# One layer of a hybrid decoder with mixture of experts, one core: last tile projected in column halves and its logits scaled late, GpSimd's end moved into the last branch, counts ahead of a table product, idle products behind a pair

## What is computed

```python
h = rmsnorm(x, g_mix)
a_b, a_c, a_x, p_x, c_a, c_g, d_u, d_v = split(h @ w_in, 8)      # 1024 -> 2048
mix = concat([short_conv(..), pooling(..), conv31(..), chunk_gating(..)])
x = x + mix @ w_out                                            # 1024 -> 1024
h = rmsnorm(x, g_ffn)
lg, le = h @ rg_w + rg_b, h @ re_w + re_b                      # 4 groups, 32 experts
g = argmax(lg);  e1, e2 = top2(le within g);  w2 = softmax(v2) * softmax(lg)[g]
x = x + sum_k w2[k] * ((silu(h @ w_gate[e_k]) * (h @ w_up[e_k])) @ w_down[e_k])
y = rmsnorm(x, g_final)
```

## Time and profile before

| | |
|---|---|
| runs, us | 647.76, 646.43, 646.13; median 646.43 |
| profiled execution, us | 649.03 |
| its span, us | 647.3 |
| mean granted clock of TensorE | 0.958 |
| busy: PE, DVE, ACT, POOL | 92%, 74%, 44%, 16% |
| chain that ended last | PE 58%, DVE 17%, DMA 2%, ACT 2%, issue 2% |

### The profile page before, as it was taken

How to read it: one execution, slowest core, us unless ns; L and a number is a source line. 1 busy time by engine, 2 the same in 40 slices (tenths; PEclk the granted TensorE clock), 3 DMA queues, 4 the chain that set the end, 5 groups by cost and what they waited for, 6 DMA issues and landing times.

```text
span 647.3 us, 10611 instructions
## 1 busy us (share of the span) xinstructions
PE 594.5 (92%) x3527; PEld 509.6 (79%) x3527; DVE 481.2 (74%) x752; ACT 283.6 (44%) x437; POOL 106.0 (16%) x150
## 2 busy tenths in 40 slices
PE   5899999999999998999999934999999999998792
PEld 3899999997898897888888724888888888885641
DVE  4947997999999678366665666878888878885287
ACT  5642112330313345322221134777777777774433
POOL 4300001000000000000000003133344444452000
PEclk9799999999999999999999955999999999999798
DMA  8660210111203103544221097799999999941595
GB/s 312 127 127 22 66 33 11 56 55 34 65 10 132 65 2 131 194 173 185 72 91 50 33 331 217 224 345 357 335 331 368 393 383 377 380 181 57 190 418 225
DMA packets 51303, 115.83 MB, mean 179 GB/s; under 512 B 8419, under 2 KB 26728, under 8 KB 50153
## 3 DMA queue, kind: packets, MB, share of 16 engines
q1 hardware_dynamic: 42757, 92.30, 41.4%
q0 software_dynamic: 6656, 17.84, 8.0%
q10 hardware_dynamic: 1828, 4.96, 2.0%
HBM read 99.23 MB, written 20.68 MB: 185 GB/s over the span
## 4 chain that ended last, share of the span: by engine, by line
PE 58%; DVE 17%; DMA 2%; ACT 2%; issue 2%; POOL 0%; SPq 0%; POOLq 0%; DVEq 0%; ACTq 0%
PE ps L1976 14%; PE ps L2094 9%; PE ps L1799 8%; PE ps L2073 5%; PE ps L2054 5%; PE ps L2072 5%; PE ps L2074 5%; PE ps L2017 2%; DVE at_mixP L1247 2%; DVE at_x L1722 2%; DVE at_hT L1206 1%; PE ps L1750 1%; DVE at_x L1707 1%; DVE at_lnsq L1432 1%; DMA at_opair_p<-scratch_out 1%
## 5 line engine op out<-in xcount | busy, mean ns | idle before, releaser
L1799 PE MATMUL ps<-at_hT,at_ring 128*128 128x384 f32 x936 | 165.7, 333 | 1.1 <-ACT at_wk L645 1.1
L1799 PEld LDWEIGHTS ps<-at_hT,at_ring 128*128 128x128 f32 x936 | 155.9, 188 | 6.5 <-issue 5.0
L1976 PE MATMUL ps<-at_hT,at_mring 128*128 128x512 f32 (+1 forms) x432 | 102.6, 393 | 1.9 <-DVE at_mring L1400 1.1
L1976 PEld LDWEIGHTS ps<-at_hT,at_mring 128*128 128x128 f32 (+1 forms) x432 | 77.3, 182 | 21.1 <-DVE at_mring L1400 1.6
L2072 PE MATMUL ps<-at_whi,at_hTm 128*128 128x256 f32 x280 | 82.0, 293 | 0.0
L2074 PE MATMUL ps<-at_whi,at_hTm_lo 128*128 128x256 f32 x280 | 79.0, 282 | 0.0
L1247 DVE SCALAR_TENSOR_TENSOR at_mixP<-at_uc,sb_par,at_mixP 128x1024 f32<-128x1024 f32 x60 | 77.3, 1289 | 2.1
L1594 DVE TENSOR_TENSOR at_hTm_lo<-ps,at_hTm 128x1024 fp32r<-128x1024 f32 x35 | 42.9, 1225 | 21.6 <-ACT at_hTm L885 21.6
L2054 PEld LDWEIGHTS ps<-sb_ident,at_xg 128*128 128x128 f32 x280 | 37.3, 190 | 24.8 <-issue 22.0
L1601 DVE TENSOR_TENSOR at_wlater_lo<-at_wlater,at_whi 128x1024 fp32r<-128x1024 f32 x40 | 49.0, 1226 | 9.7 <-ACT at_whi L893 7.5
L2072 PEld LDWEIGHTS ps<-at_whi,at_hTm 128*128 128x128 f32 x280 | 53.8, 192 | 0.2 <-issue 0.2
(11 more groups left out here) (255 smaller groups left out, 901.3 us busy)
## 6 DMA issues: line engine op xcount, KB each, us to landing
at_wlater<-in_expert_w_gate SPq DMA_DIRECT2D x20, 512.0 KB
at_wlater<-in_expert_w_up SPq DMA_DIRECT2D x20, 512.0 KB
at_wlater<-in_expert_w_down SPq DMA_DIRECT2D x20, 512.0 KB
at_raw<-in_w_in SPq DMA_DIRECT2D x16, 512.0 KB, 3.9
at_opair_p<-scratch_out SPq DMA_DIRECT2D x8, 1024.0 KB, 14.0
at_wfirst<-in_expert_w_gate SPq DMA_DIRECT2D x15, 512.0 KB
at_wfirst<-in_expert_w_up SPq DMA_DIRECT2D x15, 512.0 KB
at_wfirst<-in_expert_w_down SPq DMA_DIRECT2D x15, 512.0 KB
```

Source lines behind the costliest of these rows:

```text
L1799: mm = pe.matmul(ps[:, bank + r, 0:t1 - t0], w[:, wpart, k * P:(k + 1) * P], hT[:, hpart, k, t0:t1], start=(m, wpart, hpart) == (0, 0, 0), ...
L1976: mm = pe.matmul(ps[0:n, b + r, :], mring[:, 1 - i % 2, mpart, k * P:k * P + n], wo[:, wpart, k, r * 512:(r + 1) * 512], start=(c, mpart, ...
```

## The change

1. **Last tile in column halves.** For the last tile `project` runs all channels into the first 512 columns and then all into the second (`o_half` after the first). VectorE's `last_half` adds 512 columns to x and multiplies them with the gain, without the root; the transposes wait for `last_scaled`, the end of the second half. The logits are multiplied with the root in `route`. ScalarE makes the scaled rows for the store, in another buffer, and fills all four gather buffers behind that.
2. **VectorE's list** is written out for the end: row and column selectors are apart, and the column selectors of tile 7 stand behind the choice of the last tile.
3. **Counts** of the last tile stand ahead of the table product of tile 7 on TensorE.
4. **Rows of expert 1** are transposed into banks 5 and 6 (`rows_psum`), and its transposes no longer wait for the remainder of expert 0's rows.
5. **Last overflow block**: the branch is asked ahead of D of the block before; in it, TensorE runs half of that D, the transpose, the other half, and the last D; ScalarE copies the transpose ahead of the output.
6. **GpSimd's end**: the memset with `moe_done` stands in `all_scattered`, inside the branches.
7. **Idle products**: the last 8 of 32 wait for the pair of the sample's tile.

```diff
@@ -378 +378 @@
+def rows_psum(b):
+    n = 5 if isinstance(b, int) and b == 1 else 0
+    return ps[:, n:n + 2, :]
...
 def by_tile(flat):
@@ -537 +542 @@
     def store_h2(i):
...
-        sp.dma_start(hs[i * P:i * P + rows(i), :], wk[0:rows(i), i % 2, 0:D])\
+        sp.dma_start(hs[i * P:i * P + rows(i), :], wk[0:rows(i), 2 if i == LAST else i % 2, 0:D])\
@@ -864 +869 @@
-        if i >= LAST:
-            act.wait_ge(s["o_done"], TILES)
-            for n in range(3) if i == LAST else range(3, XG):
-                zeros = ones[:].unsqueeze(1).broadcast_to([P, KC, P])
-                do(A(xg[:, n, :].rearrange("p (k t) -> p k t", k=KC), zeros, ACT.Copy, scale=0.0),
-                   s["xg_zero"])
+    act.wait_ge(s["rs_ready"], 2 * TILES)
+    do(A(wk[0:NS, 2, 0:D], wk[0:NS, LAST % 2, 0:D], ACT.Copy, scale=rs[0:NS, 1, LAST:TILES]),
+       s["h2_ready"])
+    for n in range(XG):
+        zeros = ones[:].unsqueeze(1).broadcast_to([P, KC, P])
+        do(A(xg[:, n, :].rearrange("p (k t) -> p k t", k=KC), zeros, ACT.Copy, scale=0.0),
+           s["xg_zero"])
@@ -881 +886 @@
-        src = ps[:, 0:2, :].rearrange("p b (k t) -> p (b k) t", t=P)
+        src = rows_psum(b).rearrange("p b (k t) -> p (b k) t", t=P)
...
     def expert_whi(i, j, h):
@@ -971 +976 @@
                     with act.If(i * LAP + j + 1 < total):
...
-                    expert_out(i + NE // LAP, j - 1)
                     with act.If(i * LAP + j + 2 > total):
...
+                        expert_out(i + NE // LAP, j - 1)
...
+                    with act.Else():
+                        expert_out(i + NE // LAP, j - 1)
...
     def final_root(i):
@@ -1154 +1161 @@
+        g.memset(gcol[:, 0:1], 0).then_inc(s["moe_done"], 1)
...
     def over_from(o):
@@ -1170 +1178 @@
-    do(g.memset(gcol[:, 0:1], 0), s["moe_done"])
@@ -1473 +1480 @@
+    def last_half(h):
+        if h == 0:
+            dve.wait_ge(x_in[LAST], 32)
+            dve.wait_ge(s["o_half"], 1)
+            dve.wait_ge(s["t2_done"], LAST - 1)
+            dve.wait_ge(h2_stored[LAST % 2], 16 * (LAST // 2))
+        else:
+            dve.wait_ge(s["o_done"], TILES)
+        c = slice(h * 512, h * 512 + 512)
+        do(tt(x1[0:NS, LAST, c], x1[0:NS, LAST, c], ps[0:NS, 2 * (LAST % 2) + h, :], ALU.add),
+           s["x1_ready"] if h == 1 else None)
+        do(tt(wk[0:NS, LAST % 2, c], x1[0:NS, LAST, c], gain[0:NS, c], ALU.mult),
+           s["last_scaled"] if h == 1 else None)
     def route(i):
@@ -1480 +1502 @@
-        do(tt(lge[q, i, :], m_area(name)[q, 0:8 + NE], rb[q, :], ALU.add), s["mf_dve"])
+        if i == LAST:
+            dve.wait_ge(s["rs_ready"], 2 * TILES)
+            do(stt(lge[q, i, :], m_area(name)[q, 0:8 + NE], rs[q, 1, i:i + 1], rb[q, :],
+                   ALU.mult, ALU.add), s["mf_dve"])
+        else:
+            do(tt(lge[q, i, :], m_area(name)[q, 0:8 + NE], rb[q, :], ALU.add), s["mf_dve"])
@@ -1516 +1543 @@
-    def table_parts(i):
+    def table_rows(i):
@@ -1526 +1553 @@
+    def table_cols(i):
+        n = rows(i)
+        q = slice(0, n)
@@ -1534 +1566 @@
-    for i in range(TILES + 2):
-        if i + 1 < TILES:
-            mix_lo(i + 1)
-        if i == TILES:
-            table_parts(i - 2)
-        elif i >= 2:
+    for i in range(LAST):
+        mix_lo(i + 1)
+        if i >= 2:
...
-            table_parts(i - 2)
-        if i == LAST:
+            table_rows(i - 2)
+            table_cols(i - 2)
+        residual(i)
+        dve.wait_ge(s["rs_ready"], TILES + i + 1)
+        if i >= 2:
+            dve.wait_ge(s["t2_done"], i - 1)
+            dve.wait_ge(h2_stored[i % 2], 16 * (i // 2))
+        normed(i, 1, "h2_ready")
+        if i >= 1:
...
-        if i < TILES:
-            residual(i)
-            if i == LAST:
-                places(i - 1)
-            dve.wait_ge(s["rs_ready"], TILES + i + 1)
-            if i >= 2:
-                dve.wait_ge(s["t2_done"], i - 1)
-                dve.wait_ge(h2_stored[i % 2], 16 * (i // 2))
-            normed(i, 1, "h2_ready")
-        if 1 <= i <= TILES and i != LAST:
-            route(i - 1)
+    places(LAST - 2)
+    table_rows(LAST - 2)
+    table_cols(LAST - 2)
+    last_half(0)
+    route(LAST - 1)
+    last_half(1)
+    places(LAST - 1)
+    table_rows(LAST - 1)
+    route(LAST)
+    table_cols(LAST - 1)
+    places(LAST)
+    table_rows(LAST)
+    table_cols(LAST)
@@ -1965 +2002 @@
-        for c in range(q * KC // 4, (q + 1) * KC // 4):
+        for c in range(q % 2 * KC // 2, (q % 2 + 1) * KC // 2) if i == LAST \
+                else range(q * KC // 4, (q + 1) * KC // 4):
...
-                for r in range(2):
+                for r in (q // 2,) if i == LAST else range(2):
...
+        if i == LAST and q == 1:
+            mm.then_inc(s["o_half"], 1)
@@ -1992 +2032 @@
     def second_T(t):
...
-        pe.wait_ge(s["h2_ready"], t + 1)
+        if t == LAST:
+            pe.wait_ge(s["last_scaled"], 1)
+        else:
+            pe.wait_ge(s["h2_ready"], t + 1)
@@ -2036 +2079 @@
+    counts(LAST)
...
-    counts(LAST)
@@ -2047 +2090 @@
     def expert_T(i, j):
...
-        if not early(b, 1):
+        if not early(b, 2):
...
-            mm = pe.transpose(ps[:, k // 4, k % 4 * P:(k % 4 + 1) * P],
+            mm = pe.transpose(rows_psum(b)[:, k // 4, k % 4 * P:(k % 4 + 1) * P],
@@ -2082 +2125 @@
-    def expert_D(i, j):
+    def expert_D(i, j, halves=(0, 1)):
...
-        if not early(b, 1):
-            pe.wait_ge(s["ob_act"], b)
-            pe.wait_ge(s["ob_dve"], b)
-        pe.wait_ge(s["att_ready"], b + 1)
-        for r in range(2):
+        if 0 in halves:
+            if not early(b, 1):
+                pe.wait_ge(s["ob_act"], b)
+                pe.wait_ge(s["ob_dve"], b)
+            pe.wait_ge(s["att_ready"], b + 1)
+        for r in halves:
...
-        mm.then_inc(s["d_done"], 1)
+        if 1 in halves:
+            mm.then_inc(s["d_done"], 1)
...
     def step(i, j, first, last):
@@ -2131 +2176 @@
-                    expert_D(i + NE // LAP, j - 1)
                     with pe.If(i * LAP + j + 2 > total):
...
+                        expert_D(i + NE // LAP, j - 1, (0,))
...
+                        expert_D(i + NE // LAP, j - 1, (1,))
...
+                    with pe.Else():
+                        expert_D(i + NE // LAP, j - 1)
...
+        if n == WARM - 8:
+            pe.wait_ge(pair_in[FINAL[0]], 16)
```

More of the change, by code:

```diff
@@ L303, in build_layer @@
             "ht_free", "mixa_hi", "mixa_lo", "mix_first", "c_norm", "c_ready", "conv_ready", "mix_ready",
-            "stage_out", "mh_hi", "mh_lo", "o_done", "x1_ready", "h2_ready",
+            "stage_out", "mh_hi", "mh_lo", "o_half", "o_done", "last_scaled", "x1_ready", "h2_ready",
             "t2_done", "h2T_ready", "pads_ready", "gex_in", "gex_out", "m_onehot",
```

## The result

The changed kernel takes **644.24 us** (median of 11 runs, 642.53 to 646.86) against 647.53 (11 runs) of the kernel before on the same chip: ratio 0.9948, 95% interval 0.9931 to 0.9964. That is 3.4 us less, where 8.2 less was forecast, and outside the range (641.5 at its high end).

The account below looks back on a forecast made before the run. Two chains, before and after the TensorE-bound expert laps, were taken to set the change's worth. 3.1 + 1.0 + 2.4 + 1.8 = 8.3, less 0.1, gave -8.2 and a 638.2 us median; range 636.5 to 641.5.

Parts of the forecast that it names:

- term D: At the end, the first pair's sum follows the idle products without a gap, at full clock: -1.8 us.
- Branches: GpSimd's pause is the scatter's end, or an else arm pauses TensorE or ScalarE: 640.6, or 645.7 if three blocks pay; chance 0.10.
- The first gather runs into the loads: The earlier first gather meets expert loads not yet drained, shrinking the last-tile gain to 1 or less: 640.5; chance 0.05.
- Term A: Last tile projected in column halves, root and norm off the path, so transposes start earlier: -3.1 us.
- Term B: Expert 1's rows in other banks, so its transposes and first products come earlier: -1.0 us.
- the falling clock: Between experts 0 and 1 TensorE waits longer for VectorE and the clock drops, costing 1.5 to 2.5: 640.3; chance 0.15.
- Last overflow block: TensorE's transpose of block 34 between the halves of block 33's D: zero gain, within 0.2 us either way.
- Term C: At GpSimd's end, the memset directly after the last scatter's wait removes a 2.49 us pause: -2.4 us.

Follow-up runs that it names:

- Without the arms: The changed kernel with TensorE's and ScalarE's last overflow block written as before, without if/else; 639.30 us, ratio 0.9892.
- its later forms: The changed kernel without if/else arms, plus one expert load held (0.9869), 8 idle products before expert 0's second product transpose (0.9879), or both (0.9884).
- the idle products in the wait: 8 idle TensorE products ahead of expert 0's second product transpose, added to the kernel without if/else arms: 640.45 us; with one expert load held too, 640.54.

## Why the prediction was wrong

**The step that failed** is in term D: the idle products "are just ending" when the first pair comes, and "TensorE goes from one to the other without a gap". That moved their start with the last D, in other words it kept the 3.42 that I had read before them as a constant. It is not one: it became 6.67 when the code behind the last D grew, and the idle products, which nothing shortened, became the bound. The changed kernel's pause holds two slow branches (2.78 and 2.97) where the kernel before had one (2.55). The last column puts the loss at 2 to 3: with a long pause and 32 idle products it reads 19.33 to 20.14, with a short one and the early memset 16.42 to 17.91. Without the arms the same change stands at 0.9892 (0.9845 to 0.9938), and in its later forms with all of B, C and D at 0.9869 to 0.9884, where the forecast, 638.2 of 646.43, was 0.9873.

**Branches** was a rival at 0.10, but with the wrong mechanism: I looked for a pause at an arm, once at 640.6, or in each of three blocks that run at 645.7. It came once, at the way out, past blocks that never run. The Trainium skill, Runtime: NRT & Kernel Launch, Instruction fetch mechanics, says that a taken branch to a page that isn't held waits for its transfer; by that rule, which I had in hand, the jump over five blocks should have been costed, and the slow branches with a transfer on q8 beside each (2.78 with 593.81, 2.97 with 597.62) agree with it. What one costs the trace of the kernel before could have shown: of the 3.42 that I took as a constant, 2.55 are one branch of TensorE's sequencer, where the others take 0.34 at most.

**The first gather runs into the loads** was a rival at 0.05, bounded by 0.5. With the loads still at a DMA share near 1.0 it took 4.64 to 6.50 in nine kernels; in the three with one load held, at a share of 0.0, 4.61 to 4.94; in the four with the late gather, 4.58 to 4.88. What tells the nine apart is when the last packet of the loads (q1) begins: 2.1 to 2.5 us after the gather's issue in the three with 4.64 to 4.81, 3.2 to 4.1 in the six with 5.32 to 6.50. The runs bear the mechanism out; its price is 0 to 1.8, not 0.5, and 1.34 in the profile after, where the forecast had the loads drained at 388.5 and their last packet began at 390.06.

**Term A**, -3.1: right. Add to gather 18.18 to 14.98, -3.2.
**Term B**, -1.0: right in size (12.84 to 11.83 from transposes to transpose); the falling clock, a rival priced at 1.5 to 2.5, cost 1.5 to 2.9 where it struck. That was only with B (five of nine, none of five without), which suggests that B exposes it and doesn't prove it.
**Last overflow block**, 0 within 0.2: from D of block 33 to the last D 3.49 and not 3.20 in the timelines, so +0.3, besides the code it adds.
**Term C**, -2.4: right in size (7.84 to 5.28 from the last D to the memset), worth nothing behind the idle products, and in the kernel before worth C and D together.
**Term D**, -1.8: the sum did shrink, 5.41 to 3.45, but not by the wait. The sample's pair was there at 605.77 and the 64 passes ran in one piece. C alone brings D with it: one cause, which I had written as two edits.

Left open: how often the clock falls in unprofiled executions, and so what the idle products in the wait are worth; why it held until the logits in five kernels; and whether the distance or the place of the code makes the second slow branch.

## What to carry to other kernels

A pause before an engine's first instruction behind a long run of branches can grow when an edit adds code to the blocks, also to those that never run. Look at the rows of the engine's sequencer there: a branch that takes ten times as long as its neighbours is the pause, and no constant. When an edit makes data come earlier, look for filler work that was sized for the old arrival: here the idle products had 2 us to spare before, and none after. And test a term alone both in the old and in the new kernel: one memset was worth 0.7% in the first and nothing in the second.

## What the runs showed of the hardware

- On TensorE's way out of the branches one slow branch (2.1 to 3.0 us, the others 0.35 at most) goes with a pause of 3.0 to 3.8 us, two with 5.9 to 6.7. Some 72 instructions more in eight blocks, or 80 in the five that never run, make the second; 45 or 27 do not.
- From profile to profile the clock rose 2.6 to 9.1 us ahead of the transpose of expert 0's product. Where it rose early (5.6 and more, five profiles), it fell to 0.50 again, with a wait of TensorE of 2.2 to 3.0 us right ahead of the transpose in four of them; where it rose late, the waits were 1.0 to 1.9 and it held.
- A gather issued into running loads took 4.64 to 4.81 us when the last packet of the loads began within 2.5 us, 5.32 to 6.50 when later; 4.58 to 4.94 with none, or a few packets, left.
- A pause that is 3 us longer can cost nothing, and even keep the clock high for the work behind it.
